# Two fp32 ones sums per RMS norm in place of eight, with the squares added up on VectorE

## What is computed

```python
h = rms_norm(x, norm_mix[l]) * (1.0 + sc1) + sh1     # the mixing norm
proj = h @ w_in[l]
...
merged = jax.nn.sigmoid(gate_a) * y_a + jax.nn.sigmoid(gate_b) * y_b
x = x + gt1 * (merged @ w_o[l])

h = rms_norm(x, norm_ffn[l]) * (1.0 + sc2) + sh2     # the second norm
up_act, up_lin = jnp.split(h @ w_up[l], 2, axis=-1)
up_act = causal_dwconv(up_act, ffn_conv[l]) + ffn_conv_b[l]
x = x + gt2 * ((jax.nn.silu(up_act) * up_lin) @ w_down[l])
```

```python
def rms_norm(x, w):
    xf = x.astype(jnp.float32)
    y = xf * lax.rsqrt(jnp.mean(xf * xf, axis=-1, keepdims=True) + EPS)
    return (y * w.astype(jnp.float32)).astype(x.dtype)
```

## Time and profile before

| | |
|---|---|
| median of 3 runs | 2817.19 us (2815.6 to 2820.2) |
| profiled execution | 2816.6 us, of which the span of instructions is 2814.8 us |
| TensorE (PE) busy | 2600.1 us, 92% of the span |
| VectorE (DVE) busy | 1427.4 us, 51% |
| ScalarE (ACT) busy | 1076.0 us, 38% |
| GpSimd (POOL) busy | 909.5 us, 32% |
| mean granted clock of TensorE | 0.967 of full speed |

### The profile page before, as it was taken

The page is one execution under the profiler, slowest core; times in us unless marked ns, Lnnn a source line. Parts: engine busy times, 40 slices in busy tenths (PEclk is TensorE's granted clock), DMA queues, the critical chain, the costliest instruction groups (busy, mean ns, idle before and its releaser), DMA issues. The chain is left out here.

```text
span 2814.8 us, 33154 instructions
## 1 busy us (share of the span) xinstructions
PE 2600.1 (92%) x13041; PEld 2094.9 (74%) x13041; DVE 1427.4 (51%) x2585; ACT 1076.0 (38%) x1872; POOL 909.5 (32%) x402
## 2 busy tenths in 40 slices
PE   4988999898989999988998989999899998999998
PEld 3766768797867888856776778877788886786787
DVE  5279738653625541035994676444443304746323
ACT  3345454235332322233554522453333223336522
POOL 1432231112434444334222221134344443332343
PEclk8999999999999999989999989999999999999999
DMA  6211315634233423222131366333223333651232
GB/s 232 75 60 61 121 60 148 178 120 150 90 105 124 145 91 99 91 87 63 61 119 62 98 151 182 108 122 100 75 90 103 96 95 122 132 131 46 75 112 83
DMA packets 339838, 299.96 MB, mean 107 GB/s; under 512 B 56974, under 2 KB 319460, under 8 KB 338660
## 3 DMA queue, kind: packets, MB, share of 16 engines
q1 hardware_dynamic: 287716, 279.49, 32.0%
q10 hardware_dynamic: 51968, 18.35, 2.6%
HBM read 267.89 MB, written 29.93 MB: 106 GB/s over the span
## 5 line engine op out<-in xcount | busy, mean ns | idle before, releaser
L273 PE MATMUL ps<-hh,split 128*128 128x512 f32 x3808 | 1292.9, 407 | 52.1 <-POOL split L220 31.8
L220 POOL TENSOR_TENSOR split<-ring,split 128x1024 fp32r<-128x1024 f32 (+2 forms) x342 | 805.4, 2356 | 1458.2 <-ACT split L216 1458.1
L273 PEld LDWEIGHTS ps<-hh,split 128*128 128x128 f32 x3808 | 730.0, 192 | 223.9 <-POOL split L220 56.1
L273 PE MATMUL ps<-hl,split 128*128 128x512 f32 x1904 | 754.2, 396 | 0.0
L216 ACT ACTIVATE split<-ring 128x1024 fp32r<-128x1024 f32 (+2 forms) x342 | 347.6, 1018 | 897.1 <-PE ps L273 672.4
L273 PEld LDWEIGHTS ps<-hl,split 128*128 128x128 f32 x1904 | 366.3, 192 | 72.0 <-issue 7.4
L273 PE MATMUL ps<-split 128*128 128x512 f32 x1152 | 291.5, 409 | 10.4 <-PEq L978 8.5
L273 PEld LDWEIGHTS ps<-split 128*128 128x128 f32 x1152 | 218.8, 190 | 76.1 <-issue 19.2
L2122 PE MATMUL ps<-split 128*128 128x512 f32 x1056 | 247.5, 395 | 0.0
L2122 PEld LDWEIGHTS ps<-split 128*128 128x128 f32 x1056 | 198.2, 188 | 46.3 <-issue 5.7
L560 POOL TENSOR_TENSOR split<-ring,split 128x1024 fp32r<-128x1024 f32 x32 | 75.9, 2372 | 357.2 <-ACT split L552 357.2
(11 more groups left out here) (396 smaller groups left out, 3221.0 us busy)
## 6 DMA issues: line engine op xcount, KB each, us to landing
ring<-in_w_in_dram SPq DMA_DIRECT2D x60, 1024.0 KB, 5.3
ring<-in_w_up_dram SPq DMA_DIRECT2D x44, 1024.0 KB, 5.1
ring<-in_w_ada_dram SPq DMA_DIRECT2D x64, 512.0 KB, 3.8
ring<-in_w_in_dram SPq DMA_DIRECT2D x34, 512.0 KB, 5.2
big<-in_w_ada_dram SPq DMA_DIRECT2D x16, 1024.0 KB, 8.3
ring<-in_w_down_dram SPq DMA_DIRECT2D x16, 896.0 KB, 4.9
ring<-in_w_swa_out_dram SPq DMA_DIRECT2D x8, 1024.0 KB, 5.2
ring<-in_w_dn_out_dram SPq DMA_DIRECT2D x8, 1024.0 KB, 5.2
```

Of the source, the lines that this page charges most:

```text
L220: on.tensor_tensor(halves(pt, nk)[1], slot(n, nk)[:, :, e * P:(e + 1) * P], halves(pt, nk)[0], ALU.subtract).then_inc(low_made, 1)
L273: ins = nc.tensor.matmul(ps[bank[gt]][0:m, :], w[:, k, :], r[:, k, :], start=(k == 0 and w is w_high and r is rhs[0]), stop=(k == nk - 1 a ...
```

## The change

The ones matrix is linear in the squares, so the squares of the tiles may be added first. In both norms of each layer ACT writes the square of tile 0 into a tile of its own (`square_sum`, which is `big[:, 8, :]`, for the second norm; `mix_sum`, which is `wk[:, 10, :]`, for the mixing norm). DVE adds the squares of tiles 1 to 6 to it, each behind the addition to `x` of the tile after it. TensorE takes two ones sums at the end: one of the accumulated tile (squares 0 to 6), and one of the square of tile 7. ACT's wait for a free buffer of squares goes by DVE's sum in place of TensorE's.

```diff
--- before.py
+++ after.py
@@ -1765,7 +1765,7 @@
                 ffn_squared, ffn_summed, ffn_rs, ffn_scaled, ffn_high, ffn_low, ffn_added = (
                     sem("ffn_" + s) for s in ("squared", "summed", "rs", "scaled", "high", "low", "added"))
                 z = wk[:, 0:8, :]
-                gates = sq
+                gates, square_sum = sq, big[:, 8, :]
                 o_dn = split[:, 8:16, :], split[:, 16:24, :]
                 merged = split[:, 0:8, :], split[:, SPLIT_WK:SPLIT_WK + KD, :]
                 with nc.Block() as block:
@@ -1807,18 +1807,13 @@
                             gemm(pe, G_Z + t, (hh, hl))
                         for t in range(KD):
                             gemm(pe, G_DN + t, o_dn, ready=f_low if t == 0 else None)
-                        def total(k):
-
-                            pe.wait_ge(ffn_squared, k + 1)
-                            nc.tensor.matmul(ps[7][:, :], ones, wk[:, 8 + k % 2, :], start=(k == 0), stop=(k == KD - 1)
-                                             ).then_inc(ffn_summed, 1)
-
                         for t in range(KD):
                             gemm(pe, G_WO + t, merged, ready=m_low if t == 0 else None)
-                            if t >= 2:
-                                total(t - 2)
-                        total(KD - 2)
-                        total(KD - 1)
+                        pe.wait_ge(ffn_summed, KD - 2)
+                        nc.tensor.matmul(ps[7][:, :], ones, square_sum, start=True, stop=False)
+                        pe.wait_ge(ffn_squared, KD)
+                        nc.tensor.matmul(ps[7][:, :], ones, wk[:, 8 + (KD - 1) % 2, :], start=False, stop=True
+                                         ).then_inc(ffn_summed, 2)
 
 
                         pe.wait_ge(low_made, G_UP + 2)
@@ -1890,9 +1885,10 @@
                             if t == 1:
                                 exp_ln_tables()
                             act.wait_ge(ffn_added, t + 1)
-                            if t >= 2:
-                                act.wait_ge(ffn_summed, t - 1)
-                            nc.scalar.activation(wk[:, 8 + t % 2, :], x[:, t, :], ACT.Square).then_inc(ffn_squared, 1)
+                            if t >= 3:
+                                act.wait_ge(ffn_summed, t - 2)
+                            nc.scalar.activation(wk[:, 8 + t % 2, :] if t else square_sum, x[:, t, :], ACT.Square
+                                                 ).then_inc(ffn_squared, 1)
                         act.wait_ge(ffn_summed, KD)
                         nc.scalar.activation(wk[:, 10, :], ps[7][:, :], ACT.Ln, bias=eps, scale=1 / D).then_inc(ffn_rs, 1)
                         act.wait_ge(ffn_rs, 1)
@@ -1932,6 +1928,13 @@
                                 dve.wait_ge(m_high, t)
                                 nc.vector.tensor_tensor(merged[1][:, t - 1, :], gates[:, t - 1, :], merged[0][:, t - 1, :],
                                                         ALU.subtract).then_inc(m_low, 1)
+                        def sum_square(t):
+
+                            dve.wait_ge(ffn_squared, t + 1)
+                            if t >= 2:
+                                dve.wait_ge(ffn_summed, t - 1)
+                            nc.vector.tensor_tensor(square_sum, square_sum, wk[:, 8 + t % 2, :], ALU.add).then_inc(ffn_summed, 1)
+
                         dve.wait_ge(x_in_again, 16)
                         for t in range(KD):
                             gt = G_WO + t
@@ -1940,6 +1943,8 @@
                                                            in1=x[:, t, :], op0=ALU.mult, op1=ALU.add).then_inc(ffn_added, 1)
                             dve.wait_ge(ffn_added, t + 1)
                             nc.vector.sem_inc(evacuated[bank[gt]], 1)
+                            if t >= 2:
+                                sum_square(t - 1)
                         dve.wait_ge(ffn_rs, 2)
                         for k in range(KD + 2):
                             if k < KD:
@@ -2079,13 +2084,22 @@
                             sp.wait_ge(far_in, 16)
                             sp.wait_ge(rel_out, 16)
 
+                    mix_sum = wk[:, 10, :]
+
                     def square_down(act, k):
 
                         gt = G_DOWN + k % 4
+                        if k >= 3:
+                            act.wait_ge(mix_summed, k - 2)
+                        act.wait_ge(evacuated[bank[gt]], use[gt] + 1 + k // 4)
+                        nc.scalar.activation(mix_square(k) if k else mix_sum, x[:, k, :], ACT.Square).then_inc(mix_squared, 1)
+
+                    def sum_down(dve, k):
+
+                        dve.wait_ge(mix_squared, k + 1)
                         if k >= 2:
-                            act.wait_ge(mix_summed, k - 1)
-                        act.wait_ge(evacuated[bank[gt]], use[gt] + 1 + k // 4)
-                        nc.scalar.activation(mix_square(k), x[:, k, :], ACT.Square).then_inc(mix_squared, 1)
+                            dve.wait_ge(mix_summed, k - 1)
+                        nc.vector.tensor_tensor(mix_sum, mix_sum, mix_square(k), ALU.add).then_inc(mix_summed, 1)
 
                     @block.scalar
                     def _(act):
@@ -2124,16 +2138,15 @@
                                                                        stop=(k0 + k == FT - 1 and w is w_low))
                                         ins.then_inc(part_made, 1)
                                         k = 4 * i + 2 * pair
-                                        if j == 0 and e == 0 and k:
-                                            mix_total(pe, k - 1)
-                                        if j == 2 and e == 1:
-                                            mix_total(pe, k)
                                         if j == 1 and e == 1 and k == 4:
                                             if l + 1 < DEPTH:
                                                 turn_rows(pe)
                                             else:
                                                 turn_rows_2(pe)
-                        mix_total(pe, KD - 1)
+                        pe.wait_ge(mix_summed, KD - 2)
+                        nc.tensor.matmul(ps[7][:, :], ones, mix_sum, start=True, stop=False)
+                        pe.wait_ge(mix_squared, KD)
+                        nc.tensor.matmul(ps[7][:, :], ones, mix_square(KD - 1), start=False, stop=True).then_inc(mix_summed, 2)
 
                     @block.vector
                     def _(dve):
@@ -2154,6 +2167,8 @@
                                     nc.vector.scalar_tensor_tensor(out=xs, in0=ps[bank[gt]][:, :].unsqueeze(1),
                                                                    scalar=mod[:, ds(40 + 4 * i + m, 1)], in1=xs,
                                                                    op0=ALU.mult, op1=ALU.add).then_inc(evacuated[bank[gt]], 1)
+                                    if 4 * i + m >= 2:
+                                        sum_down(dve, 4 * i + m - 1)
 
 
                 clear_all()
```

## The result

The changed kernel takes 2802.1 us, the median of 4 runs (2800.5 to 2807.3), against 2817.7 us before in the same set of runs: the ratio is 0.9942, 95% interval 0.9928 to 0.9956, so -16.3 us (-20 to -12). The prediction was 2801.0 us (range 2796 to 2808), 16.2 us less. Two further sets, on two chips, each with its own runs of the kernel before, gave 0.9945 (0.9929 to 0.9961) and 0.9949 (0.9935 to 0.9962).

What follows compares the result with a forecast made beforehand. TensorE, busy 92% of the span, was taken to bound the kernel. Removed ones sums (-19.8 us) and longer norm ends (+3.6 us) made -16.2 us: from 2817.2 to 2801.0 us, range 2796 to 2808.

Steps and rivals of the forecast that it cites:

- Sums between products, 0.90 us each, 22 of them on the path: Second norm and down projection: removing five and six ones sums a layer saves 0.90 us each, -19.8 us over two layers.
- DVE's sums between products cost nothing: Both norms: 20 of the 24 added DVE additions run while DVE would be idle, so they cost nothing.
- The ends, +3.6 us: End of each norm: one more ones sum on the path, +0.87 us (second norm) and +0.9 (mixing norm), two layers.
- The first rival: Second norm's end: the last DVE sum begins behind GpSimd's low part and waits, +2.4 us a norm, 2805.9 us; chance 9%.
- The second rival: Norm ends: TensorE's clock falls in the idle time before the ones sums, +6.9 us, 2807.9 us; chance 8%.
- well under the 4.3 us: Argument against the clock falling: PE idles some 1.7 us before the sums, where the clock fell after 4.3 us idle.
- The third: Between products: the removed sums were not on the path and a wait fills their place, 2817 us; chance 3%.
- The fourth: Between products: DVE's sums delay GpSimd's low parts until their feed sets the pace, e.g. +28.8 us, 2829.8 us; chance 2%.
- What I called the easiest way to be wrong: After the changed stages: the clock's falls come at other moments of the work.
- The 1 or 2 us that the prediction allowed: Behind the norm: the start of the existing clock fall may shift by 1 or 2 us either way, allowed below 2801.

Runs made afterwards that it cites:

- `three_sums`: Changed kernel, but DVE adds only squares 1 to 5 to square 0 and TensorE takes three ones sums per norm; 2793.8 us, 0.9916 against before.
- `doubled_sums`: Kernel before, with a second ones product behind each of the second norm's five ones sums between products; one execution took 2831.1 us.

## Why the prediction was right

- **Sums between products, 0.90 us each, 22 of them on the path: right.** -9.01 and -10.78 us, together -19.8, as the sum had it. That the first sums behind the last product are worth nothing fits as well: `three_sums`, with three there in each norm, ends within 0.07 us of before.
- **DVE's sums between products cost nothing: right.** They took 691 to 694 ns in the second norm (L1929's own figure) and 681 to 684 in the down projection, and even a second operation of 2.9 us behind them cost nothing.
- **The ends, +3.6 us: right in sum (+3.4), a little off in both terms.** Second norm +0.95 in place of +0.87: the new sum waits for the addition ahead of it, and its gap is 0.22 and not the 0.14 of L1929. Mixing norm +0.73 in place of 0.9: nothing separates the sum from the addition there, it ends before the last square, and PE starts 0.1 us earlier than the pair of before would have.
- **The first rival** did not come, with a margin of 0.15 us and not 0.24. Its price was right for the sum (2.83 us, 0.55 behind GpSimd) and too low for the norm, since I had priced it and the second rival as if they came apart: +3.8 us (7.54 against 3.74), not +2.4.
- **The second rival** did not come: a pause of 1.76 us left the clock alone in all profiles of the changed kernel. After pauses of 4.16 and 4.50 us (four in all) the sums ran at the lower level, wholly or from their second record on, and so they did after one of two pauses of 2.29 us. So "well under the 4.3 us" was a weaker reason than it looked; that 1.76 us never did it (10 pauses in 5 profiles) is what the runs show.
- **The third and fourth rivals.** The third falls with `doubled_sums` (no wait of more than 0.04 us fills the place of a sum). The fourth falls with the profile after: GpSimd's low parts beside a sum took 2.65 to 2.79 us, about 0.3 more than without, as forecast, where over 5.0 were needed, and no tile of `w_o` came late.
- **What I called the easiest way to be wrong**, the clock at other places, moved single executions of the changed kernel from 2796.8 to 2808.9 us. The median stood. The 1 or 2 us that the prediction allowed for where the fall behind the norm begins were too few: a fall some 1.3 us earlier came with 285.7 in place of 280.2 us in layer 0 and 277.9 in place of 274.0 in layer 1.
- **Luck.** That the medians differ by 16.3 us where 16.2 were forecast is in part luck, since the interval is -20 to -12. What confirms the sum is the -16.4 us of the stretches.

## What to carry to other kernels

A reduction over tiles on TensorE costs a product for each tile; where it stands between products of a stage that TensorE paces, adding the tiles up first on an engine that is idle gives back each of them, here 0.90 us apiece. What ends the chain should not be moved: leave the last tiles on the engine that is waiting anyway, so that the added-up tile is done early and its product runs in the pause, which is what three sums do and two do not. And read such a change from stretches between the same events, not from one span: the span of the first profile said -9.4 us, the stretches -16.4, and the runs agree with the latter.

## What I had not expected of the hardware

- Stretches at full clock repeat to 0.04 us over executions and chips, while whole executions of one program spread over 10 us and more (2814.2 to 2825.0 for the kernel before, 23 runs). In the up projection the differences come from stretches at the lower clock: behind pauses of PE of 2.2 to 3 us they come or stay away, and at the one of 4.3 us they begin earlier or later. The stretch before the changed code, 770.7 to 777.9 us long, is the same code in all of these kernels.
- A DVE operation held up by GpSimd (2.8 to 2.9 us for 0.69) costs more than its own delay when PE waits for it: with a pause of 4.16 us the clock fell each time, and the two sums after it took 1.4 us longer in layer 0 and 1.2 in layer 1.
